# Taking a norm's second weight chunk through the tiles once, with both sums open

## What is computed

```python
# first stack, layer i
u = rms_norm(h, norm_mix_g[i])
proj = u @ w_in[i]                  # q, k, v, pool, convolution and gate columns
q1 = rms_norm(q[..., 0, :], q_norm_g[i])   # per head of 64; the same for q2, k1, k2
...
m = rms_norm(h, norm_mlp_g[i])
h = h + jnp.square(jax.nn.relu(m @ w_up[i])) @ w_down[i]
...
# second stack: rmsnorm(x, g) * (1 + scale) + shift ahead of each of these
x = x + g2 * sq_relu_mlp(modulate(x, norm2_g[i], sh2, sc2), mlp_w1[i], mlp_w2[i])
z = short_conv(modulate(x, norm1_g[1], sh1, sc1) @ h_w_in, conv_w, conv_b)
```

## Time and profile before

| | us |
|---|---|
| three runs | 3511.6, 3512.2, 3517.08 |
| median | 3512.2 |
| the profiled execution's own time | 3514.61 |
| its span, first to last instruction | 3512.4 |
| busy: PE, DVE, ACT, POOL | 3302.5, 2051.1, 1213.9, 638.9 |
| mean granted clock of TensorE | 0.969 |

### The profile page before, as it was taken

The page is one execution under the profiler, slowest core; times in us unless marked ns, Lnnn a source line. Parts: engine busy times, 40 slices in busy tenths (PEclk is TensorE's granted clock), DMA queues, the critical chain, the costliest instruction groups (busy, mean ns, idle before and its releaser), DMA issues.

```text
span 3512.4 us, 36794 instructions
## 1 busy us (share of the span) xinstructions
PE 3302.5 (94%) x15132; PEld 2649.6 (75%) x15132; DVE 2051.1 (58%) x2655; ACT 1213.9 (35%) x1647; POOL 638.9 (18%) x487
## 2 busy tenths in 40 slices
PE   7999999999999999999988999979999888699998
PEld 5877777888787777888876676767778767577887
DVE  6645557664765555777556556555455577754443
ACT  3233432224433433322432333333333433232222
POOL 0000000000100002999710000002333022310000
PEclk9999999999999999999999899989999999899999
DMA  2222134542222214454221010022323222122222
GB/s 102 87 84 84 60 138 180 192 180 88 93 78 88 78 66 146 180 192 180 102 78 35 15 43 1 25 79 105 117 104 136 108 84 72 60 84 96 96 96 72
DMA packets 55623, 342.94 MB, mean 98 GB/s; under 512 B 5985, under 2 KB 7329, under 8 KB 18209
## 3 DMA queue, kind: packets, MB, share of 16 engines
q1 hardware_dynamic: 54080, 337.98, 26.9%
q10 hardware_dynamic: 1376, 2.62, 0.2%
HBM read 328.00 MB, written 12.58 MB: 97 GB/s over the span
## 4 chain that ended last, share of the span: by engine, by line
PE 69%; DVE 14%; POOL 10%; ACT 4%; issue 2%; DMA 0%; DVEq 0%; ACTq 0%; POOLq 0%
PE PS L262 68%; POOL FA L271 9%; DVE FA L279 2%; DVE wl L271 2%; PE PS L265 2%; DVE SC L279 1%; DVE SC L288 1%; ACT wh L268 1%; DVE SC L271 1%; ACT SC L268 1%; DVE PB L271 1%; DVE FA L288 1%; DVE UL L271 1%; DVE PS L271 1%; DVE FA L271 1%
## 5 line engine op out<-in xcount | busy, mean ns | idle before, releaser
L262 PE MATMUL PS<-UH,wh 128*128 128x512 f32 x2072 | 837.4, 404 | 39.2 <-DVE wl L271 20.9
L271 DVE TENSOR_TENSOR wl<-raw,wh 128x2048 fp32r<-128x2048 f32 (+2 forms) x255 | 566.8, 2223 | 458.3 <-ACT wh L268 458.3
L262 PE MATMUL PS<-UL,wh 128*128 128x512 f32 x2072 | 815.5, 394 | 0.0
L262 PE MATMUL PS<-UH,wl 128*128 128x512 f32 x2072 | 815.2, 393 | 0.0
L262 PE MATMUL PS<-RH,wh 128*128 128x512 f32 (+2 forms) x1688 | 669.7, 397 | 60.9 <-DVE wl L271 35.9
L262 PE MATMUL PS<-RL,wh 128*128 128x512 f32 (+2 forms) x1688 | 658.8, 390 | 0.0
L262 PE MATMUL PS<-RH,wl 128*128 128x512 f32 (+2 forms) x1688 | 658.6, 390 | 0.0
L268 ACT ACTIVATE wh<-raw 128x2048 fp32r<-128x2048 f32 (+2 forms) x255 | 454.4, 1783 | 322.1 <-PE PS L262 318.8
L262 PEld LDWEIGHTS PS<-UH,wh 128*128 128x128 f32 x2072 | 394.5, 190 | 157.5 <-issue 28.1
L262 PEld LDWEIGHTS PS<-UL,wh 128*128 128x128 f32 x2072 | 394.8, 191 | 85.3 <-issue 6.7
L262 PEld LDWEIGHTS PS<-UH,wl 128*128 128x128 f32 x2072 | 394.0, 190 | 84.0
(11 more groups left out here) (191 smaller groups left out, 3273.8 us busy)
## 6 DMA issues: line engine op xcount, KB each, us to landing
raw<-in_wall SPq DMA_DIRECT2D x224, 1024.0 KB, 4.8
FA<-in_wmod SPq DMA_DIRECT2D x48, 1024.0 KB, 4.9
raw<-in_wall SPq DMA_DIRECT2D x29, 512.0 KB, 3.5
kspec<-FA SPq DMA_DIRECT2D x8, 1024.0 KB, 7.3
FA<-kspec SPq DMA_DIRECT2D x8, 1024.0 KB, 5.7
PB<-in_window SPq DMA_DIRECT2D x16, 256.0 KB, 4.2
raw<-in_wall SPq DMA_DIRECT2D x8, 272.0 KB, 2.7
Hs<-in_xT ACTq DMA_DIRECT2D x4, 512.0 KB, 10.4
```

What stands on the lines that cost most here:

```text
L262: return self.put(self.eng and self.eng.matmul(out, w, x, start=start, stop=stop, skip_group_check=True))
L271: return self.put(self.eng and self.eng.tensor_tensor(out, a, b, op))
```

## The change

`from_x` gets two arguments. With `by_tile` it takes both outputs' banks, waits for each tile once and issues the three matmuls of the first output and the three of the second on it, as `first_x` does. `between` is called after each tile. It is used for the second chunk of the five norms in `TWICE`: `up` 1 of n = 7 and 9, `qk` 1 of both layers, `hw` 1. In the layers head sum 0 is now issued after tile 4 and head sum 1 after tile 6; head sum 2 moves behind output 4, where head sum 3 follows it.

```diff
--- before.py
+++ after.py
@@ -548,8 +548,21 @@
                 three(out, w, x, i == 0, i == n - 1)
             p.then_inc("sum", key)
 
-        def from_x(tag, keys, frees, n, of=range(8)):
+        def from_x(tag, keys, frees, n, of=range(8), by_tile=False, between=None):
             p.wait_ge("w_lo", tag)
+            if by_tile:
+                for key, fr in zip(keys, frees):
+                    take(key, *fr, of=of)
+                for k in range(8):
+                    for e in x_made(n, k):
+                        p.wait_ge(*e)
+                    for m, key in enumerate(keys):
+                        three(ps(key), pair(tag, 256 * k + 128 * m), X(n, k), k == 0, k == 7)
+                        if k == 7:
+                            p.then_inc("sum", key)
+                    if between is not None:
+                        between(k)
+                return
             for m, key in enumerate(keys):
                 take(key, *frees[m], of=of)
                 group(key, ps(key), [(pair(tag, 256 * k + 128 * m), X(n, k), x_made(n, k)) for k in range(8)])
@@ -668,8 +681,12 @@
             for q in range(4):
                 for j in range(4):
                     ks, first = (2 * j, 2 * j + 1), q == 0 and j == 0
-                    (first_x if first else from_x)(("up", M, q, j), [("up", M, q, k) for k in ks],
-                                                   [[("r_x" if M < 2 or first else "r_sq", (M, q, k))] for k in ks], n)
+                    tag, keys = ("up", M, q, j), [("up", M, q, k) for k in ks]
+                    frees = [[("r_x" if M < 2 or first else "r_sq", (M, q, k))] for k in ks]
+                    if first:
+                        first_x(tag, keys, frees, n)
+                    else:
+                        from_x(tag, keys, frees, n, by_tile=n in TWICE and q == 0 and j == 1)
                     if M == 2:
                         filters(8 * q + j)
                 for j in range(4):
@@ -690,12 +707,16 @@
                 if i == 0:
                     first_x(("qk", l, 0), [("qk", l, k) for k in ks], [[("qk_x", (l, k))] for k in ks], n)
                     continue
+                if i == 1:
+                    from_x(("qk", l, 1), [("qk", l, k) for k in ks], [[("qk_x", (l, k))] for k in ks], n, by_tile=True,
+                           between=lambda t: head_sum(l, t // 2 - 2) if t in (4, 6) else None)
+                    continue
                 for m, k in enumerate(ks):
                     key = ("qk", l, k)
                     take(key, ("qk_x", (l, k)))
                     group(key, ps(key), [(pair(("qk", l, i), 256 * t + 128 * m), U(t), u_made(n, t)) for t in range(8)])
-                    if i == 1 and m == 0:
-                        head_sum(l, 0)
+                    if i == 2 and m == 0:
+                        head_sum(l, 2)
                     head_sum(l, k - 1)
             for j in range(2):
                 p.wait_ge("w_lo", ("v", l, j))
@@ -1048,7 +1069,7 @@
                 if j == 0:
                     first_x(tag, keys, [[("hw_x", (0, m))] for m in range(2)], 8)
                 else:
-                    from_x(tag, keys, [[("hw", (j, m))] for m in range(2)], 8, of=low)
+                    from_x(tag, keys, [[("hw", (j, m))] for m in range(2)], 8, of=low, by_tile=j == 1)
 
             def signal(s):
                 for t4 in range(4):
```

## The result

Six runs took 3524.8 to 3532.4, median **3526.4 us**, beside six of the kernel before on the same chip with a median of 3516.3 (3511.6 to 3521.0). The ratio is **1.0034 (95% interval 1.0023 to 1.0045)**: slower by 12.0 (11.8 between the means, 3527.5 against 3515.7; 10.1 between the medians). The profiled execution took 3529.05 (span 3526.9), 14.4 more than that of before.

A forecast was written before the change was run, and what follows sets the result against it. VectorE's order was taken to set the layers' end, despite TensorE's 94% busy share. Layer delays of 7.2 plus clock terms 1.1, 1.5, 0.2 and 0.2 made 10.2, added to the median 3512.2: 3522 us, range 3511 to 3528.

The forecast's parts named there:

- head sum 0 blocks TensorE at tile 4: Layers' second chunk: head sum 0 waits for ScalarE's square, TensorE idling some 3.3 in layer 0, 3.8 in layer 1.
- the early read of head 2: Layers: VectorE's eviction of head 2 at 58.10, inside the second output's matmuls, would be lost under joint opening.
- Norms 7 and 9: Second chunks there: TensorE finishes earlier but waits longer for VectorE's weight halves, worth 0 apart from clock.
- Rival A: Norms 7, 8, 9: work behind really waits for TensorE, 4.8 gained each; 3505, or 3488 if all five pay; chance 0.10.
- B (no block): Layers: head sum 0's operand is there at tile 4, or later slack absorbs the delay; 3512 to 3514, chance 0.12.
- C (the clock in full): Clock falls fully at both layers' blocks and at head sums 7; 3530, chance 0.06.
- the carry-over to the median: Last step: the profiled execution is 2.4 above the median 3512.2, to which the sum is added, giving 3522.
- The sum: Whole kernel: 7.2 of layer delay plus 1.1, 1.5, 0.2 and 0.2 of clock, 10.2 slower.
- The delay in layer 0: Layer 0: head 2's eviction at 61.4 against 58.10, +3.3, plus 1.1 of clock.
- Layer 1: Layer 1: head 2's sum at 949.8 against 945.77, +3.9 after a wait of 0.17, plus 1.5 of clock.
- Norm 9's 0.2 of clock: Chunk after norm 9 still starts at 3168.01; clock effect -0.4 to +1.2, taken as 0.2.
- Norm 8: Transposes behind the chunk wait for VectorE's convolutions: worth 0, and 0 to 1 for a clock falling sooner.

The follow-up runs named there:

- run 1: Changed kernel with head sums 0 and 1 put behind the whole second chunk, both outputs still open together: ratio 1.0007 to the kernel before.
- run 5: Kernel of run 1 with heads 2 to 7 evicted by ScalarE instead of VectorE, behind the root of head k-2: ratio 1.000.
- run 5b: Kernel before, two passes everywhere, with heads 2 to 7 evicted by ScalarE instead of VectorE, behind the root of head k-2: ratio 0.9991.
- run 4: Kernel before with one more unused reciprocal (3.35 us) on VectorE ahead of head 2's eviction in each layer: ratio 1.0022.
- Run 3: Kernel before, two passes kept, with only head sums 0 and 1 moved behind tiles 4 and 6 of the first output's pass: ratio 1.0029.
- run 2: Kernel before with the change at norms 7, 8 and 9 only, layers as before: ratio 1.0003.
- run 7: Kernel before with weight halves of a later chunk made right behind norms 7 and 9: ratio 0.9952.
- run 8: Kernel of run 1 plus ScalarE's evictions, early weight halves, and ScalarE's root straight from PSUM without VectorE's scaling step: 3490.2 us, ratio 0.9931.
- run 9: Kernel before, two passes, with ScalarE's evictions, root straight from PSUM and early weight halves, as in run 8: 3498.3 us, ratio 0.9953.

## Why the prediction was right, and where it was wrong

**The direction and the place: right.** Hiding the second output is worth nothing in the layers (runs 1, 5 and 5b), because VectorE's order sets their end; head sum 0 blocks TensorE at tile 4, and starts where it started before (56.10, by the trace after); the sum of head 2 is the one that is late, and its delay passes whole to head sum 7 (5.05 and 5.05 in layer 0, run 4 by a delay of known size). Run 3 gives a loss of the same size without the joint pass, though with more clock in it; run 1 gives the joint pass without the loss in the layers' head sums. One cause that the prediction gave beside the block isn't one by itself: the early read of head 2 was held to be lost by opening the two sums together, but run 1 has both open and evicts head 2 at 60.09 - 1.96 = 58.13 against 58.10. Norms 7 and 9: 0, as said, with waits 4.1 longer. Rival A (weight waits that aren't VectorE's) falls by runs 2 and 7, B (no block) by the 3.73, C (the clock in full) by layer 1's full clock.

**The time: too low by 4.4, and the step that failed is the last one, the carry-over to the median.** The sum was 10.2 for a change that measured 12.0 by the ratio, 10.1 by the two medians. I took 2.4 off the profiled execution to come down to the median of three runs, 3512.2, and added the sum there. But three runs spread over 5.5 don't fix a level: three more beside the changed kernel took 3516.2, 3516.3 and 3521.0, which makes the median of all six 3516.3, and later medians of the same kernel were 3514.6 (30 runs), 3516.1 (17) and 3516.7 (9). Set against 3516.3, 3522 says +5.7, little more than half of what I had worked out and half of what was measured. The sum on the profiled execution's own 3514.6 would have been 3524.8. The range, 3511 to 3528, held the result; the forecast's own, 3519 to 3526, missed it by 0.4. That the sum, 10.2, lies so near the 10.1 between the medians is in part luck: single terms below were off by up to 1.5 and cancel, and 1.8 of the profiled difference belongs to no term.

**The terms:**

- The delay in layer 0 was put at 3.3 and 1.1 of clock, 4.4; it was 5.05. The eviction at 61.4 was worked out for a full clock and came at 63.15. Of these 1.75 some 0.1 is the path itself: at full clock, in layer 1, it took 5.44 from head sum 0 to the eviction (957.85 - 952.41) where I had 5.3. The clock took the other 1.6 of the 2.8 that I had worked out for a full fall, where I had set 1.1. The idle stretch was 3.73 and not 3.3, since nine and not twelve matmuls ran at 0.43; that changed nothing, as head sum 0 can't start before its square.
- Layer 1: 3.9 and 1.5 of clock at the block. It was 4.0 at head sum 7 and no clock at the block; but 1.5 went behind head sum 7, where I had 0.2 for both layers. The total, 10.55 against 10.0, was nearly right by two errors that cancel: I gave the longer idle stretch the greater risk, and it was the one without.
- Norm 9's 0.2 of clock: the wait ends where it did (14.31 and 14.30), and 0.25 was lost in the first matmuls behind it (14.56). But run 4, which changed nothing there, lost as much (9.08 to 9.33), so it can't be put down to the change. Norm 8: the shift is 12.80 ahead of its second chunk, 12.80 at the transposes and 13.62 seven microseconds later, within the 0 to 1; run 5b, which has two passes there, moved as much (0.36 to 1.34).

The Trainium skill, "Perfetto Trace Analysis", section "Identifying Performance Opportunities", says to optimise the engine with the highest occupancy first. The prediction went by the 94% of its matmuls; for TensorE that section asks for the busy share of the weight loads (and the share of peak arithmetic) instead, and the former is 75% here against VectorE's 58%, so TensorE it is by either. Yet hiding 5.5 of its work five times over brought nothing (runs 1 and 2). Under "Optimization Strategy" the same section also says to find the gaps on that engine and what blocks it, and to make that dependency start sooner or complete faster; run 7, which does just that to two gaps, agrees with 0.9952. Neither rule says which gap is worth anything: the gaps between tiles that the change filled were TensorE's too. Here that was decided by whether TensorE waits once more at the end of the stretch.

## What to carry to other kernels

Before hiding work of the busiest engine, look for its wait at the end of the stretch: if it waits there already (1.55 at 94.18), time saved ahead of it only lengthens that wait, until the other engine's chain is made shorter; then the same edit pays (4.8 per layer in runs 8 and 9). Where an engine runs its program in a fixed order, an instruction whose operand comes from another engine should stand where that operand is already made: placed sooner, it holds up all that is behind it. Runs 1 and 3 show this for a head sum on TensorE; for an eviction behind a root on ScalarE it is read from run 5's timeline, and run 8, which changed the root as well, fits it. And add a sum of a profiled execution to that execution's own time, with the scatter of the runs as its error.

## What the hardware showed unexpectedly

The granted clock doesn't follow from the length of the idle stretch ahead: behind 3.73 it fell to 0.50, behind 3.69 it stayed at 1.00 (layers 0 and 1 of the changed kernel); behind 2.06 it stayed at full in layer 0 of the same kernel, fell to 0.66 over three microseconds behind 2.06 in its layer 1, and behind 2.08 in layer 0 of run 1, but not in layer 1 of run 1; behind the 2.07 at head sum 7 of run 4 it stayed at full in both layers. Half is the lower of the engine's two levels, 1.2 of 2.4 GHz. Ahead of the 3.73 the engine had just come out of half clock (nine matmuls some 0.43 apart from 45.71 on, those behind them at full), ahead of the 3.69 it had run at full; for the places at 2.06 to 2.08 I found no such difference. What decides it stays open. The stretches, ahead of the 3.73 and of the 3.69 and behind the 2.06 of layer 0 after, then behind the 2.08 in run 1:

```profile
45.70:49.30 3.60, 3.59 (x9) 2.83 (x10) 3.46 (x4) 1.26 (x2) 1.65 (x2) 0.50 0.00 0
943.00:949.00 6.00, 5.36 (x21) 3.41 (x19) 5.86 (x7) 3.84 (x6) 2.59 (x2) 1.00 0.00 0
...
101.40:104.40 3.00, 3.00 (x20) 2.52 (x21) 2.52 (x1) 2.25 (x2) 0.00 (x0) 1.00 0.00 0
```

```profile
96.20:99.20 3.00, 3.00 (x12) 2.49 (x13) 2.55 (x1) 2.21 (x2) 0.00 (x0) 0.64 0.00 0
```

The first 44 us, in which nothing was changed, scattered by up to 5.8 between profiled executions (43.55 before, 49.39 in run 5b). That is half of the effect under study, and only the shift across each stretch keeps it out.
